# A shorter opening, and attention heads placed between parts of the cross values, in a two-block transformer kernel

## The reference

```python
y = rmsnorm(h, norm_mix_g[l]) @ w_in[l]
q = partial_rotary(y[..., 0:D_ATT].reshape(B, S, ATT_HEADS, HEAD_DIM))
k = partial_rotary(y[..., D_ATT:2 * D_ATT].reshape(B, S, ATT_HEADS, HEAD_DIM))
v = y[..., 2 * D_ATT:3 * D_ATT].reshape(B, S, ATT_HEADS, HEAD_DIM)
att = dilated_sliding_attention(q, k, v).reshape(B, S, D_ATT)
conv = conformer_conv(...)          # gated, 31 taps per channel, layer norm over channels, silu
h = h + jnp.concatenate([att, conv], axis=-1) @ w_out[l]

xq = rmsnorm(h, norm_x_g[l]) @ w_xq[l]
mn = rmsnorm(mem, norm_mem_g[l])
xk, xv = mn @ w_xk[l], mn @ w_xv[l]   # cross keys and cross values: need only mem
```

## Time and profile before

| | us |
|---|---|
| median of 3 runs | 1485.74 (1483.89 to 1492.4) |
| profiled execution, its own time | 1483.83 |
| its span, first to last instruction | 1482.0 |
| TensorE matmuls busy | 1400.0 (94%) |
| VectorE busy | 1089.7 (74%) |
| ScalarE busy | 830.9 (56%) |
| chain that ended last: TensorE, VectorE, ScalarE | 82%, 14%, 2% |
| mean granted clock of TensorE | 0.975 of full speed |

### The profile page before, as it was taken

One profiled execution on the slowest core, in us unless ns is written; L12 is line 12 of the kernel. 1 busy time (PEld: TensorE's weight loads), 2 busy tenths in 40 slices (PEclk: granted clock), 3 DMA queues, 4 the chain that ended last, 5 costly groups with the idle time before them and its releaser, 6 DMA issues.

```text
span 1482.0 us, 21894 instructions
## 1 busy us (share of the span) xinstructions
PE 1400.0 (94%) x8173; PEld 1222.9 (83%) x8173; DVE 1089.7 (74%) x1582; ACT 830.9 (56%) x1145; POOL 56.1 (4%) x60
## 2 busy tenths in 40 slices
PE   4997999999999999999999998988999999999997
PEld 4885587989988987899999997767888888888886
DVE  3889565656557876655555888767898898898986
ACT  3444354543435754453434484435787787787784
POOL 0000000000002130000000013010000000000000
PEclk9998899999999999999999999997999999999998
DMA  7555042555654520455555450117998988988983
GB/s 272 173 169 170 0 143 86 171 192 179 198 182 133 170 73 1 141 169 175 197 177 193 130 171 29 58 43 284 369 334 308 376 313 312 372 322 298 378 320 120
DMA packets 162964, 292.76 MB, mean 198 GB/s; under 512 B 6832, under 2 KB 78924, under 8 KB 162764
## 3 DMA queue, kind: packets, MB, share of 16 engines
q1 hardware_dynamic: 162336, 291.08, 56.8%
q10 hardware_dynamic: 556, 0.67, 0.1%
HBM read 290.69 MB, written 1.05 MB: 197 GB/s over the span
## 4 chain that ended last, share of the span: by engine, by line
PE 82%; DVE 14%; ACT 2%; issue 1%; ACTq 0%; POOL 0%; DVEq 0%; POOLq 0%
PE bank L532 23%; PE bank L534 22%; PE bank L533 22%; DVE weights_split L1869 4%; DVE arena L2050 3%; PE bank L1169 2%; PE bank L990 1%; PE bank L981 1%; PE bank L1242 1%; PE bank L996 1%; PE bank L666 1%; PE bank L646 1%; PE bank L1008 1%; PE bank L1219 1%; DVE arena L2389 1%
## 5 line engine op out<-in xcount | busy, mean ns | idle before, releaser
L1869 DVE TENSOR_TENSOR weights_split<-weights,weights_split 128x1024 fp32r<-128x1024 f32 (+4 forms) x266 | 304.3, 1187 | 179.0 <-ACT weights_split L1395 178.9
L1395 ACT ACTIVATE weights_split<-weights 128x1024 fp32r<-128x1024 f32 (+4 forms) x266 | 258.5, 1022 | 282.1 <-PE bank L534 281.4
L532 PE MATMUL bank<-features_split,weights_split 128*128 128x256 f32 x912 | 262.7, 288 | 13.7 <-DVE weights_split L1869 4.7
L533 PE MATMUL bank<-features_split,weights_split 128*128 128x256 f32 x912 | 260.2, 285 | 0.0
L534 PE MATMUL bank<-features_split,weights_split 128*128 128x256 f32 x912 | 260.1, 285 | 0.0
L532 PE MATMUL bank<-weights_split,features_split 128*128 128x512 f32 (+3 forms) x560 | 217.1, 388 | 8.5 <-DVE features_split L1876 3.6
L534 PE MATMUL bank<-weights_split,features_split 128*128 128x512 f32 (+3 forms) x560 | 213.5, 381 | 0.0
L533 PE MATMUL bank<-weights_split,features_split 128*128 128x512 f32 (+3 forms) x560 | 213.4, 381 | 0.0
L532 PEld LDWEIGHTS bank<-features_split,weights_split 128*128 128x128 f32 x912 | 177.3, 194 | 17.4 <-DVE weights_split L1869 6.2
L533 PEld LDWEIGHTS bank<-features_split,weights_split 128*128 128x128 f32 x912 | 177.3, 194 | 0.5
L534 PEld LDWEIGHTS bank<-features_split,weights_split 128*128 128x128 f32 x912 | 177.2, 194 | 0.0
(11 more groups left out here) (362 smaller groups left out, 2267.0 us busy)
## 6 DMA issues: line engine op xcount, KB each, us to landing
weights<-in_moe_gate_dram SPq DMA_DIRECT2D x26, 1024.0 KB, 6.6
weights<-in_moe_up_dram SPq DMA_DIRECT2D x24, 1024.0 KB, 6.7
weights<-in_moe_down_dram SPq DMA_DIRECT2D x24, 1024.0 KB, 7.3
weights<-in_w_in_dram SPq DMA_DIRECT2D x20, 1024.0 KB, 5.2
weights<-in_w_up_dram SPq DMA_DIRECT2D x16, 1024.0 KB, 5.2
weights<-in_w_down_dram SPq DMA_DIRECT2D x16, 1024.0 KB, 4.9
weights<-in_w_out_dram SPq DMA_DIRECT2D x12, 1024.0 KB, 5.0
weights<-in_ffn_gate_dram SPq DMA_DIRECT2D x11, 1024.0 KB, 5.3
```

What stands on the lines that cost most here:

```text
L532: pe.matmul(ps, lhs(0), rhs(0), start=start, stop=False, skip_group_check=shared)
L533: pe.matmul(ps, lhs(0), rhs(1), start=False, stop=False, skip_group_check=shared)
L1395: do(act.activation(split_flat(j)[:, 0, part], raw_flat(j)[:, part], ACT.Copy), "hi", j, b)
L1869: do(dve.tensor_tensor(split_flat(j)[:, 1, part], raw_flat(j)[:, part], split_flat(j)[:, 0, part].bitcast(F32), ALU.subtract), "lo", j)
```

## The change

Two things are changed, both in the first 180 us.

**Opening.** ScalarE issues only the first row tile (the norms' gains, 7 transfers) before its work. A one-element square (of `NHALF`) follows, then the squares of x, the high halves of slots 0 and 1, and only then the other 12 row transfers, ahead of `features_high`. TensorE turns the first row tile alone before x, and the other two between slots 0 and 1. VectorE makes the low half of slot 0 only, copies the first 72 columns, goes through gain and features, and makes the low half of slot 1 behind them, followed by the copy of the other columns.

**Heads.** The cross values' slots 14 to 17 are taken out from before the heads. Each is used in two parts of 12 matmuls (one row tile each), and `between(s)` of step s = 0 to 7 runs one part. The last of the four cross key slots (13) comes after the turning of q and k. ScalarE makes the high half of slot 15 before the heads and those of 16 to 19 in `between` at s = 2, 4, 6, 8, and copies the cross values out at s = 3, 4, 7, 8. VectorE does two convolution steps less before mem is normalised, and after the rotation only three low halves and 20 steps; the low halves of slots 15 to 19 come at s = 0, 2, 4, 6, 8 of the heads, and two steps of the convolution at each s from 0 to 9.

```diff
@@ TensorE
-                pe.wait_ge(rows_in, 16 * 19)
+                def vector_columns(part, tiles):
+                    ps = open_bank("cols", part)
+                    at = 0
+                    for i in tiles:
+                        n = (72, 124, 94)[i]
+                        mm = pe.transpose(ps[:, at:at + n], GR[0:n, i, :], ident[0:n, 0:n])
+                        at += n
+                    mm.then_inc(*cpe.mark("filled", "cols", part))
+
                 pe.wait_ge(ident_in, 16)
...
+                pe.wait_ge(norm_rows_in, 16 * 7)
+                vector_columns(0, (0,))
...
                 for b in range(2):
                     features_out("g", HT, "g", b)
+                    if b == 0:
+                        pe.wait_ge(rows_in, 16 * 12)
+                        vector_columns(1, (1, 2))
                     features_out("a", HT, "a", b)
...
-                for i in range(4):
+                for i in range(3):
                     features_out("xk", MT, "xk", i)
-                for i in range(2):
-                    tokens_out("xv", MT, 512, i)
                 pe.wait_ge(*after("rotated"))
...
+                features_out("xk", MT, "xk", 3)
                 pe.wait_ge(*after("read", "qkT", 3))
                 pe.wait_ge(*after("read", "v", 0, 1))
+                cross_slot = {}
+
+                def cross_values(s):
+                    if s >= 8:
+                        return
+                    i, r, t = s // 4, s // 2 % 2, s % 2
+                    if t == 0:
+                        cross_slot[i, r] = weights("xv")
+                    j, w = cross_slot[i, r]
+                    ps = open_bank("xv", i, t) if r == 0 else bank_of["xv", i, t]
+                    for k in range(4):
+                        mm = matmul3(ps[:, :], lambda z: MT[:, z, 4 * r + k, t * P:(t + 1) * P],
+                                     lambda z: w[:, z, k, :], r == 0 and k == 0, r == 1 and k == 3)
+                    if r == 1:
+                        mm.then_inc(*cpe.mark("filled", "xv", i, t))
+                        cpe.also("slot", j)
+                    elif t == 1:
+                        mm.then_inc(*cpe.mark("slot", j))
...
-                attention(0, AH, scores1, pair_outs("att_o", (), V))
+                attention(0, AH, scores1, pair_outs("att_o", (), V), between=cross_values)
@@ ScalarE
+                vector_rows(0, norm_rows_in)
+                act.wait_ge(*after("nhalf"))
+                do(act.activation(SM[:, 15, 0:1], NHALF[:, 0:1], ACT.Square))
                 act.wait_ge(x_in, 32)
                 sumsq(0, X)
                 high(2)
+                vector_rows(1, rows_in)
+                vector_rows(2, rows_in)
                 features_high(0, HT, T1)
...
-                for i in range(4):
+                for i in range(3):
                     high(1)
                     copy_out(XKT[:, 2 * i:2 * i + 2, :], two(psum("xk", i)), "xk", i)
-                for i in range(2):
-                    high(2)
-                    for t in range(TT):
-                        copy_out(XV[:, t, i * 512:(i + 1) * 512], psum("xv", i, t)[:, :], "xv", i, t)
                 act.wait_ge(*after("heads_selected"))
                 for b in range(4):
                     copy_out(QKT[:, 2 * b:2 * b + 2, :], two(psum("qkT", b)), "qkT", b)
-                attention(0, AH)
+                copy_out(XKT[:, 6:8, :], two(psum("xk", 3)), "xk", 3)
+                high(1)
+
+                def cross_values(s):
+                    if s in (2, 4, 6, 8):
+                        high(1)
+                    if s in (3, 4, 7, 8):
+                        i, t = s // 4 - (s % 4 == 0), 1 - s % 2
+                        copy_out(XV[:, t, i * 512:(i + 1) * 512], psum("xv", i, t)[:, :], "xv", i, t)
+
+                attention(0, AH, cross_values)
@@ VectorE
                 rows_norm(0, X)
-                low(2)
-                dve.wait_ge(*after("filled", "cols"))
-                do(dve.tensor_copy(COL[:, :], psum("cols")[:, 0:NCOLS]), "read", "cols")
+                low(1)
+                dve.wait_ge(*after("filled", "cols", 0))
+                do(dve.tensor_copy(COL[:, 0:72], psum("cols", 0)[:, 0:72]), "read", "cols", 0)
                 own()
...
+                turned(0, "norm_mix_g", 0, HT, T1)
+                low(1)
+                dve.wait_ge(*after("filled", "cols", 1))
+                do(dve.tensor_copy(COL[:, 72:NCOLS], psum("cols", 1)[:, 0:NCOLS - 72]), "read", "cols", 1)
+                own()
...
-                    conv_taps(4 if i < 2 else 2)
+                    conv_taps(3 if i < 2 else 2)
...
-                for i in range(8):
-                    low(1)
-                    conv_taps(5 if i < 6 else 4)
-                assert taps_done == [TAPS, TAPS]
+                for i in range(4):
+                    if i < 3:
+                        low(1)
+                    conv_taps(5)
...
-                attention(0, AH, 0.125, flat(logc), outs1)
+                def beside_heads(s):
+                    if s in (0, 2, 4, 6, 8):
+                        low(1)
+                    if s < 10:
+                        conv_taps(2)
+
+                attention(0, AH, 0.125, flat(logc), outs1, between=beside_heads)
+                assert taps_done == [TAPS, TAPS]
```

More of the change, by code:

```diff
@@ L359, in program @@
         x_in, mem_in, rows_in, table_in = sem("x_in"), sem("mem_in"), sem("rows_in"), sem("table_in")
-        select_in = sem("select_in")
+        select_in, norm_rows_in = sem("select_in"), sem("norm_rows_in")
         ident_in, moe_out = sem("ident_in"), sem("moe_out")
@@ L672, in pair_outs @@
                     return outs
-                pe.wait_ge(rows_in, 16 * 19)
-                pe.wait_ge(ident_in, 16)
-                ps = open_bank("cols")
-                at = 0
-                for i, n in enumerate((72, 124, 94)):
-                    mm = pe.transpose(ps[:, at:at + n], GR[0:n, i, :], ident[0:n, 0:n])
-                    at += n
-                mm.then_inc(*cpe.mark("filled", "cols"))
+                def vector_columns(part, tiles):
[6 more added lines that the diff above has]
+                    mm.then_inc(*cpe.mark("filled", "cols", part))
+                pe.wait_ge(ident_in, 16)
+                pe.wait_ge(norm_rows_in, 16 * 7)
+                vector_columns(0, (0,))
                 turn_norm(0)
@@ L1352, in _, with vector_rows @@
             def _(act):
-                for i, tile in enumerate(ROWS):
+                def vector_rows(i, arrived):
                     at = 0
-                    for name, n in tile:
+                    for name, n in ROWS[i]:
                         src = A[name]
@@ L1359, in _ @@
                             for z in range(2):
-                                act.dma_start(GR[at:at + n, i, z * HD:(z + 1) * HD], src).then_inc(rows_in, 16)
+                                act.dma_start(GR[at:at + n, i, z * HD:(z + 1) * HD], src).then_inc(arrived, 16)
                             at += n
@@ L1368, in _ @@
                             src = src.rearrange("a (r p) -> (a r) p", p=P)
-                        act.dma_start(GR[at:at + n, i, :], src).then_inc(rows_in, 16)
+                        act.dma_start(GR[at:at + n, i, :], src).then_inc(arrived, 16)
                         at += n
```

1 line of the change is left out of this document (removed).

## The result

| | before | after |
|---|---|---|
| median of 20 runs each | 1485.76 us (1478.79 to 1492.4) | 1490.7 us (1489.41 to 1498.7) |
| ratio after to before | | 1.0044 (95%: 1.003 to 1.0057) |
| span of the profiled execution | 1482.0 | 1488.9 |
| mean granted clock in it | 0.975 | 0.972 |

The changed kernel is slower by 0.44%, some 5 us of the median and 6.9 us of the two profiled spans. I explain the 6.9, and come to the medians at the end.

A forecast was written before the change was run, and what follows sets the result against it. TensorE bounds the kernel nearly everywhere, except the opening and the VectorE-limited stretch from 95 to 178. A later channel mean read (2.1 us) plus clock falls (8.5) gave 10.6 on 1483.83: 1494.4 us, range 1482 to 1503.

The forecast's parts named there:

- head 0's scores read: VectorE's start on the first attention head: at 118.4, 25 us earlier than before.
- schedule from there to the read, full clock: From the first head's scores to VectorE's channel mean read at 180.7, without clock losses: 62.3 us.
- five falls of the clock: TensorE at half pace after idling at the first turn, three head pairs and the mean: 8.5 us together.
- behind the read: Everything after VectorE's channel mean read: same work in same order, a constant shift to the end.
- Opening: Start up to TensorE's first projection: projection 0.3 us later, plus two transposes of 0.3 us, sum +0.6 us.
- Up to the first head: From 95.22, VectorE does 3 low parts and 20 convolution steps, so the head starts at 118.4.
- Even halves: Even head steps: VectorE waits 2.7 us for ScalarE's high half before its low part; 8.7 us each.
- Odd halves: Odd head steps: next scores wait on TensorE behind turn, output and cross values; 5.4 us each.
- Clock: TensorE idling in the new heads drops its clock from 2.4 to 1.2 GHz, 1.7 us lost per fall.
- the clock holds: Rival: TensorE stays busy enough, only the first turn or the mean falls; 1488 us, chance 0.27.
- the half pace lasts: Rival: half pace holds through each odd half, five falls cost 3.4 us each; 1503 us, chance 0.16.
- The filling: Rival: high halves come ahead of the exponentials, even halves take 6.0 us, TensorE's idling goes; 1475 us, chance 0.12.

The follow-up runs named there:

- idle_filled: Changed kernel plus matmuls with unused results in TensorE's waits, no wait removed; median 1482.01 us, 0.9996 of before.
- opening_rows_first: Against `opening_alone`: ScalarE issues all 19 rows ahead of everything, the rest of the new opening kept; run once, 1484.13 us.
- heads_alone: Changed kernel with the opening taken back to that of before, the new heads kept; median 1495.38 us, 1.0076 of before.
- high_earlier: Changed kernel with ScalarE's high halves of slots 16 to 19 at s = 1, 3, 5, 7 instead of 2, 4, 6, 8; 1478.36 us, 0.9969 of before.
- opening_alone: Changed kernel with the heads taken back to those of before, the new opening kept; median 1476.36 us, 0.9964 of before.

## Why the prediction was right, and where it was wrong

The kernel got slower, as forecast, and 1490.7 lay in the range, 3.7 us under my 1494.4. The change itself was less than the 10.6 us forecast: 6.9 in the spans, 4.9 in the medians. The median is just inside the 0.5% that I had called no change (to 1491.2; I gave that 0.38, and slower 0.54), and the interval of the ratio, 1.003 to 1.0057, holds that border. That the sum came out as near as it did is in part luck, by errors of both signs:

| term | forecast | measured | difference |
|---|---|---|---|
| head 0's scores read | 118.4 | 114.10 | -4.3 |
| schedule from there to the read, full clock | 62.3 | 63.2 (`idle_filled`) | +0.9 |
| five falls of the clock | 8.5 | 9.8 | +1.3 |
| behind the read | 0 | -1.6 | -1.6 |
| sum | 10.6 | 6.9 (spans) | -3.7 |

- **Opening: wrong, sign and size.** Forecast +0.6, measured -4.2. The step that failed is "ScalarE ends them at 16.6, and then issues the 12 postponed rows". The issues were priced right, 3.9 us against my 3.8 to 4.7, but placed behind the activations instead of beside them; and the second slot, which I held at 14.6 whatever the rows do, came at 13.0. That the second low half lies beside matmuls was right, and I take it for most of the 2.9 us of `opening_rows_first`, the largest part of the gain. Of the 4.8 us between the two, 4.4 were there at the rotation (91.45 against 95.8) and 4.3 at head 0.
- **Up to the first head: right.** With the old opening it came at 118.18 (`heads_alone`), for which I had 118.4 less 0.6, 117.8. That the two steps taken out earlier bring nothing is borne out nearly: TensorE's wait for the normalised mem near 75, behind them, was 0.94 us in after and 1.18 before, 0.2 us less.
- **Even halves: right.** 8.7 forecast, 8.6 measured, ScalarE's wait 2.59 for 2.7, and `high_earlier` shows its cause.
- **Odd halves: right in kind, small by 0.45.** 5.4 forecast, 5.85 at full clock. The 5.4 was TensorE's work alone; its turn starts 0.14 us after the read from which the half is counted (131.68 and 131.82 in `high_earlier`), and the other 0.3 lie between its instructions and VectorE's next read. Two such halves are 0.9 too much, the three even ones 0.3 too little, and the rest of the walk was 0.3 longer.
- **Clock: right in number of falls, somewhat small in size.** 1.7 each forecast; 1.5 and 1.6 in the odd halves, 1.7 at the mean, but 2.5 at the first turn and before the last low half, where the half pace held on through a whole set of cross values. The Trainium skill (TensorE: Matmul & The Clock Gate, "HAM oscillation") tells of matmul bursts between waits of which each starts throttled. After the three waits of 3.2 us here the clock was at half pace each time, but one of the three bursts (151.78) began at full pace. The two waits of 2.1 us are where the traces don't decide: one fell, in before, and one didn't, in after.
- **Behind the read: not forecast.** I had a constant shift, and called a distance that changes behind the read a sign of being wrong; it did change. The missing fall at 194 gives 1.6 back.
- **The rivals.** That the clock holds is out, five falls are in the trace. That the half pace lasts is out in the heads of after, where no fall cost 3.4; that it can last is seen in before (139 to 163) and in `high_earlier` (946 to 960). The filling works only in another order: its mechanism, "as soon as ScalarE has the high half done before VectorE has negated the maximum", is what `high_earlier` does.

## What to carry to other kernels

When work of two kinds is laid between each other, follow the shared engines in program order: one split placed a step too late stopped VectorE, through it TensorE, and through that the clock, and moving one line brought 16 us at the read. Price a DMA issue by what stands behind it on its engine, not by what runs before it. And a fall of the clock is a term of its own: give each idle time of TensorE that the schedule makes a price beside its length, and test that term with matmuls that nobody reads before the order is blamed for it; but size such a filling to the gap, since one that was 14 matmuls too long made the mean start 2.3 us later.

## What the runs showed of the hardware

- ScalarE's DMA issues began at the same time as an activation that precedes them (12.98), and in the middle of a pair of activations (16.04 in one begun at 14.84), and twelve of them took 3.9 us (12.98 to 16.87).
- Postponing 12 small row transfers went with a 1 MB slot being there at 12.0 to 13.0 in nine traces, instead of 13.9 and 14.7 in two (and by 13.8 in a third).
- TensorE's clock was not a function of the wait ahead alone: 2.11 us before and a fall, 2.10 us after and none; 1.37 us and then half pace for over 14 us with TensorE busy all the while, and the same 1.37 us in another kernel with no fall. What the difference is, these runs don't tell.
- A fall near 74 was in ten of the twelve kernels' traces and not in before and after. Between 74 and the rotation it cost `opening_alone` 1.7 us (4.3 us ahead of before, then 2.6) and `heads_alone` 1.3 (1.0 ahead, then 0.3 behind). A difference of that size between two profiled executions is no effect of an edit until the granted clock of both has been compared.
